# One maximum, one scaling and one reciprocal for the two heads of a pair in the grouped attention, with both divisions on ScalarE

## The chip, the cores and the metric

One core of one Trainium2 chip runs the whole program. The metric is the time of one launch in microseconds on the device, the median of several runs. TensorE (PE in the views) multiplies, VectorE (DVE) does elementwise work and reductions, ScalarE (ACT) does activations, GpSimd (POOL) has elementwise work of its own, and the queue of SyncE (SP) issues DMAs. Each engine runs its own instructions in order and meets the others through semaphores.

## The reference

Two residual stacks run on one sequence of 512 tokens of width 1024. Each of the first stack's two layers projects the normalised input to `z`, and mixes it in three ways side by side: grouped attention (8 query heads, 2 key heads, width 64), a gated recurrence in both directions, and a convolution of 31 taps. The parts that matter here, cut short:

```python
for l in range(DEPTH):                       # DEPTH = 2
    h = rms_norm(x, norm_mix[l])
    z = h @ w_in[l]
    q_a, k_a, v_a, ..., a_c, g_c = split(z)
    o_att = block_attention(q_a, k_a, v_a)   # softmax(q k^T / 8) v, no mask, each query block of 128 against 512 keys
    o_hg  = hgrn2_bidirectional(...)
    o_cv  = conformer_conv(a_c, g_c, conv_w[l], ...)   # 31 taps along the sequence, then norm and silu
    x = x + concat(o_att, o_hg, o_cv) @ w_out[l]
    x = x + square(relu(rms_norm(x) @ w_mlp_in[l])) @ w_mlp_out[l]
```

The second stack (gated feed-forwards, a latent attention called MLA and a dilated attention) follows and is not touched by the change.

## The kernel before

Activations lie transposed in SBUF, 128 features by 512 tokens a tile. Every weight is loaded in float32, split into a high part (ScalarE, `split_hi`, L413, `w_hi`) and a low part (VectorE, `split_lo`, L422, `w_lo`), and each product is three matmuls (L444, or L452 where the result has tokens on the partitions). Weights come in units through a ring of four slots.

In a mixer layer the last eight units of the projection are multiplied with other work woven between their matmuls. The function `mixer_at` writes this out by hand: 128 points, one behind each contraction step of a unit, and at each point a list of small steps. TensorE, ScalarE and VectorE each run through the same list and do their own share of every step, in that order. From point 38 to 127 the list holds the grouped attention, from 36 to 109 the convolution: per half of the channels (`t`) one gating product and 31 taps on VectorE (L1226 and L1228, a multiply-add over up to 512 columns into `conv_sum`). `split_lo` calls stand at fixed points too. At point 111 TensorE sums the convolution over the channels (L1096, `csum`), which waits for the last tap.

The attention goes in pairs of heads: 4 pairs of heads times 4 query blocks are 16 pairs per layer, numbered 0 to 15. `pair_steps` gives the order for pair `j`: `scores j`, `values j-2`, the two turns of pair `j-1`, `divide j`. For a pair,
- **scores**: TensorE writes the 128x512 scores of head 0 into bank 4 and of head 1 into bank 5 (L857), once the exponentials of the pair ahead have read them. VectorE takes each head's row maximum into `std` (L919) and scales it into `row_stats` (L921); ScalarE takes each head's exponential with its row sum into `gqa_probs` (L893);
- **divide**: VectorE inverts the sum of the second head and of the first (L928), ScalarE multiplies the second head's probabilities by the inverse (L902), VectorE the first head's (L933);
- **turn** (one per head): TensorE transposes the probabilities (L868), ScalarE copies them out into `gqa_probs_t` (L910);
- **values**: TensorE multiplies them with the values (L878); behind every fourth pair VectorE stores the result (L959, L961).

Each instruction is followed by a wait for its own end. The buffers `gqa_probs` are four, two pairs' worth. GpSimd meanwhile weighs rows of `w_mod` (L520 to L532). The MLA attention calls the same step functions with `mla_bufs`.

Of the kernel before, what the change touches and what calls it, by code (L numbers as in the profile page):

```python
# [14 lines left out]
P = 128  # L15
L = 512
D = 1024
DT = D // P
NB = L // P
# [183 lines left out]
def build(nc, io):  # L203
    ctx = ExitStack()
    with ctx:
# [58 lines left out]

        banks = [ctx.enter_context(nc.psum_tensor(f"bank{i}", [P, L], F32)) for i in range(8)]

# [618 lines left out]
        def att_act_step(act, pairs_, bufs, kind, i):  # L885
# [10 lines left out]
            elif kind == "divide":  # L896
                it = pairs_[i]["items"][1]
                act.eng.wait_ge(inv_ready.sem, inv_ready.next(act))
                for n, (_, k, c0, _) in enumerate(it["segs"]):
                    c, part = it["stat"] + n, bufs["pr"][(2 * i + 1) % 4][:, c0:c0 + k.shape[-1]]  # L900
                    signal = pn_act if n == len(it["segs"]) - 1 else act.step
                    act.eng.activation(part, part, ACT.Identity, scale=RS[:, c:c + 1]).then_inc(signal.sem, signal.add())  # L902
                    act.eng.wait_ge(signal.sem, signal.made)
            elif kind == "turn":
                j, y = divmod(i, 2)
                n = pairs_[j]["n"]
                act.eng.wait_ge(t_ready.sem, t_ready.next(act))
                if y == 0:
                    act.eng.wait_ge(pv_twin.sem, pv_twin.next(act, lag=1))
                act.eng.activation(turned_probs(bufs, j, y)[:, 0:n], turn_bank(bufs, j, y)[:, 0:n], ACT.Copy).then_inc(pt_ready.sem, pt_ready.add())  # L910
                act.eng.wait_ge(pt_ready.sem, pt_ready.made)

        def att_dve_step(dve, pairs_, bufs, kind, i, store):
            if kind == "scores":
                for y, it in enumerate(pairs_[i]["items"]):
                    segs, c = it["segs"], it["stat"]
                    dve.eng.wait_ge(s_ready.sem, s_ready.next(dve))
                    for n, (_, k, c0, _) in enumerate(segs):
                        dve.eng.tensor_reduce(STD[:, 8 + n:9 + n], banks[4 + y][:, c0:c0 + k.shape[-1]], AX.X, ALU.max).then_inc(dve.step.sem, dve.step.add())  # L919
                        dve.eng.wait_ge(dve.step.sem, dve.step.made)  # L920
                    dve.eng.tensor_scalar(NM[:, c:c + len(segs)], STD[:, 8:8 + len(segs)], -pairs_[i]["scale"], None, ALU.mult).then_inc(nmax_ready.sem, nmax_ready.add())  # L921
                    dve.eng.wait_ge(nmax_ready.sem, nmax_ready.made)
            elif kind == "divide":
                first, second = pairs_[i]["items"]
# [41 lines left out]
        def sync_all(who, name):  # L966
# [5 lines left out]
            else:  # L972
# [4 lines left out]
                else:  # L977
# [7 lines left out]
        gqa_bufs = {"pr": [at(f"gqa_probs{i}", a, [P, L]) for i, a in enumerate((u_at + 10 * K, u_at + 12 * K, u_at + 14 * K, u_at + 6 * K))],  # L985
                    "pt": [at(f"gqa_probs_t{i}", u_at + 24 * K + 2 * K * i, [P, L]) for i in range(4)], "late": ATT_HEADS * NB // 2 - 2, "one": 12}
        CONV = [at(f"conv_sum{t}", u_at + 28 * K + 2 * K * t, [P, L]) for t in range(2)]
# [905 lines left out]
        def ffn_dve(dve, i, s):  # L1893
            for part in range(3):
# [3 lines left out]
                if (i, s, part) == (1, 1, 2):  # L1898
# [10 lines left out]
        mla_bufs = {"pr": [at(f"mla_probs{i}", a, [P, L]) for i, a in enumerate((h_at + 24 * K, h_at + 26 * K, h_at + 28 * K, u_at + 30 * K))],  # L1909
                    "pt": [at(f"mla_probs_t{i}", e_at + 20 * K + 2 * K * i, [P, L]) for i in range(2)], "late": 3 * MLA_HEADS, "one": 3 * MLA_HEADS}  # L1910
        KR = at("mla_key_rope", h_at + 30 * K, [P, L])
# [928 lines left out]
```

## Time and profile before

| | |
|---|---|
| median of 3 runs | 3871.47 us (3863.55 to 3876.67) |
| profiled execution, its own time | 3871.41 us |
| its span | 3869.6 us |
| mean granted TensorE clock | 0.97 |
| TensorE busy | 3669.3 us (95%) |
| VectorE busy | 2142.9 us (55%) |
| ScalarE busy | 1350.7 us (35%) |
| GpSimd busy | 860.9 us (22%) |
| chain that ended last, shares by engine | PE 77%, DVE 17%, ACT 3%, issue 3% |

The last row follows the chain of work that ended last from its end to its start and says on which engine it ran. The shares are averages over a long program; the two mixer stages, where the change lies, are read by themselves in the rows below.

### The profile page before, as it was taken

Reading aid. Unit: us, or ns where it says so; the run is one execution under the profiler, and the core shown is the slowest. Engines: PE = TensorE matmul, PEld = TensorE weight load, DVE = VectorE, ACT = ScalarE, POOL = GpSimd, SP = SyncE. Lnnn points to the kernel's source line nnn. Section 1 sums busy time; section 2 is a strip of 40 time slices with the busy share of each in tenths; the row PEclk is TensorE's granted clock in tenths of the full one; section 3 lists DMA queues with packets and bytes.
Section 4 is the critical chain, followed back from the end, with each engine's and each line's share of the span. In section 5 each row is a group of like instructions: output and inputs, shape, how many; then the busy total and the mean of one; then the engine's idle time right before and its main releaser. Section 6 shows DMA issues by size and latency. Waiting matters only on the chain.

```text
span 3869.6 us, 48060 instructions
## 1 busy us (share of the span) xinstructions
PE 3669.3 (95%) x19016; PEld 2954.2 (76%) x19016; DVE 2142.9 (55%) x2923; ACT 1350.7 (35%) x1795; POOL 860.9 (22%) x688
## 2 busy tenths in 40 slices
PE   8888999988899999999899999999989999989998
PEld 6567888756688878887667888788868778777887
DVE  5977444487844454447567434633564655655334
ACT  4553323356333232223673222222233333332222
POOL 2200655330055526552222640000000000000000
PEclk8989999999999999999899999999999999999999
DMA  5211655421155556663224653233322122122331
GB/s 152 67 42 39 163 144 142 113 63 42 50 144 143 140 118 152 147 148 83 52 61 102 154 131 98 75 100 98 98 74 85 61 74 85 61 66 76 98 98 66
DMA packets 564250, 377.76 MB, mean 98 GB/s; under 512 B 37297, under 2 KB 561162, under 8 KB 564026
## 3 DMA queue, kind: packets, MB, share of 16 engines
q1 hardware_dynamic: 564026, 374.69, 36.6%
q8 instruction: 151, 2.47, 0.3%
q14 instruction: 73, 0.60, 0.1%
HBM read 372.45 MB, written 2.17 MB: 97 GB/s over the span
## 4 chain that ended last, share of the span: by engine, by line
PE 77%; DVE 17%; ACT 3%; issue 3%; SPq 0%; DMA 0%; DVEq 0%; ACTq 0%
PE bank L444 61%; PE bank L452 3%; DVE conv_sum L1228 3%; PE bank L487 2%; DVE w_lo L422 2%; DVE std L919 1%; PE bank L481 1%; PE bank L857 1%; PE bank L482 1%; DVE hgrn_scores L1408 1%; DVE norm_tmp L1665 1%; PE bank L2292 1%; DVE norm_tmp L1659 1%; DVE X L1661 1%; DVE H_lo L1671 1%
## 5 line engine op out<-in xcount | busy, mean ns | idle before, releaser
L444 PE MATMUL bank<-H_hi,w_hi 128*128 128x512 f32 x2384 | 969.4, 407 | 4.9 <-DVE w_lo L422 1.7
L444 PE MATMUL bank<-H_hi,w_lo 128*128 128x512 f32 x2384 | 933.7, 392 | 0.0
L444 PE MATMUL bank<-H_lo,w_hi 128*128 128x512 f32 x2384 | 933.0, 391 | 0.0
L422 DVE TENSOR_TENSOR w_lo<-w_raw,w_hi 128x2048 fp32r<-128x2048 f32 (+3 forms) x285 | 662.8, 2326 | 150.5 <-ACT w_hi L413 142.6
L413 ACT ACTIVATE w_hi<-w_raw 128x2048 fp32r<-128x2048 f32 (+3 forms) x285 | 528.9, 1856 | 308.5 <-DMA w_raw<-in_ffn_w_up 131.5
L520 POOL TENSOR_TENSOR w_mod_raw<-w_mod_raw,silu_c 128x1024 f32<-128x1024 f32 x144 | 284.9, 1978 | 1337.4 <-DMA w_mod_raw<-in_w_mod 1291.8
L444 PEld LDWEIGHTS bank<-H_hi,w_hi 128*128 128x128 f32 x2384 | 449.0, 188 | 140.8 <-issue 49.3
L444 PE MATMUL bank<-U_hi,w_hi 128*128 128x512 f32 x1376 | 540.7, 393 | 3.8 <-DVE note L963 3.7
L444 PE MATMUL bank<-U_hi,w_lo 128*128 128x512 f32 x1376 | 536.8, 390 | 0.0
L444 PE MATMUL bank<-U_lo,w_hi 128*128 128x512 f32 x1376 | 536.4, 390 | 0.0
L444 PEld LDWEIGHTS bank<-H_hi,w_lo 128*128 128x128 f32 x2384 | 448.9, 188 | 96.8 <-issue 0.3
L444 PEld LDWEIGHTS bank<-H_lo,w_hi 128*128 128x128 f32 x2384 | 449.7, 189 | 90.8 <-issue 6.7
L1802 DVE TENSOR_TENSOR U_hi<-silu_gate,bank 128x512 fp32r<-128x512 f32 x88 | 60.5, 688 | 509.8 <-PE bank L444 500.1
L444 PEld LDWEIGHTS bank<-U_hi,w_hi 128*128 128x128 f32 x1376 | 259.0, 188 | 58.6 <-issue 4.4
L444 PEld LDWEIGHTS bank<-U_hi,w_lo 128*128 128x128 f32 x1376 | 258.7, 188 | 54.1
L444 PEld LDWEIGHTS bank<-U_lo,w_hi 128*128 128x128 f32 x1376 | 259.1, 188 | 52.7
L1789 ACT ACTIVATE silu_gate<-bank 128x512 f32<-128x512 f32 x88 | 52.8, 600 | 705.4 <-PE bank L444 701.0
L522 POOL TENSOR_TENSOR w_mod_raw<-w_mod_raw 128x512 f32<-128x512 f32 x144 | 214.1, 1487 | 11.3
L524 POOL TENSOR_TENSOR w_mod_raw<-w_mod_raw 128x256 f32<-128x256 f32 x144 | 160.5, 1115 | 11.3
L481 PE MATMUL bank<-H_hi,w_hi 128*128 128x512 f32 x320 | 135.9, 425 | 21.9 <-ACT H_hi L1637 12.0
L816 ACT ACTIVATE mid<-bank 128x512 f32<-128x512 f32 x64 | 38.4, 600 | 296.2 <-PE bank L444 275.4
L774 DVE TENSOR_TENSOR X<-X,bank 128x512 f32<-128x512 f32 x64 | 44.0, 688 | 171.1 <-PE bank L444 170.5
(366 smaller groups left out, 4696.7 us busy)
## 6 DMA issues: line engine op xcount, KB each, us to landing
w_mod_raw<-in_w_mod SPq DMA_DIRECT2D x576, 128.0 KB, 5.7
w_raw<-in_ffn_w_gate SPq DMA_DIRECT2D x88, 512.0 KB, 4.0
w_raw<-in_ffn_w_up SPq DMA_DIRECT2D x88, 512.0 KB, 5.4
w_raw<-in_dil_w_in SPq DMA_DIRECT2D x36, 1024.0 KB, 5.1
w_raw<-in_w_mlp_in SPq DMA_DIRECT2D x32, 1024.0 KB, 6.0
w_raw<-in_w_mlp_out SPq DMA_DIRECT2D x32, 1024.0 KB, 5.5
w_raw<-in_ffn_w_down SPq DMA_DIRECT2D x32, 1024.0 KB, 5.0
w_raw<-in_w_in SPq DMA_DIRECT2D x16, 1024.0 KB, 5.5
```

Source lines behind the costliest of these rows:

```text
L413: act.eng.activation(WH[u % SLOTS][:, 0:n], RAW[u % SLOTS][:, 0:n], ACT.Copy).then_inc(hi_done.sem, hi_done.add())
L422: dve.eng.tensor_tensor(WL[u % SLOTS][:, 0:n], RAW[u % SLOTS][:, 0:n], WH[u % SLOTS][:, 0:n].bitcast(F32), ALU.subtract).then_inc(lo_done. ...
L444: mm = pe.eng.matmul(bank[0:m, :], w[:, k, c0:c0 + m], r[:, k, :], start=(k == 0 and i == 0), stop=(k == kt - 1 and i == 2))
L452: mm = pe.eng.matmul(bank[:, jb * m:(jb + 1) * m], r[:, k, b * P:(b + 1) * P], w[:, k, c0:c0 + m], start=(k == 0 and i == 0), stop=(k == k ...
L481: pe.eng.matmul(banks[place][0:m, :], wh[:, k], rh[:, k, :], start=(k == 0), stop=False)
L487: mm = pe.eng.matmul(banks[place][0:m, :], w[:, k], r[:, k, :], start=(k == 0 and i == 0 and not halves), stop=(k == kt - 1 and w is wh an ...
L520: pool.eng.tensor_tensor(w[:], w[:], CSIL[:, 8 * part:8 * part + 8].unsqueeze(2).to_broadcast([P, DT, P]), ALU.mult).then_inc(pool.step.se ...
L522: pool.eng.tensor_tensor(w[:, 0:4], w[:, 0:4], w[:, 4:8], ALU.add).then_inc(pool.step.sem, pool.step.add())
L524: pool.eng.tensor_tensor(w[:, 0:2], w[:, 0:2], w[:, 2:4], ALU.add).then_inc(pool.step.sem, pool.step.add())
L1228: ins = ve.scalar_tensor_tensor(CONV[t][:, c0:c1], Z[:, ZA + t, c0 + s:c1 + s], w, CONV[t][:, c0:c1], ALU.mult, ALU.add)
L1789: act.eng.activation(SG[u % 2][:], bank[:], ACT.Silu).then_inc(free.sem, free.add())
L1802: dve.eng.tensor_tensor(UH[:, t, :], SG[u % 2][:], bank[:], ALU.mult).then_inc(dve.step.sem, dve.step.add())
```

## The change

Banks 4 and 5 become one PSUM tensor `BOTH` of 128 x 2 x 512, whose halves keep their places in the list of banks. For the grouped attention (`joint` true; the MLA attention keeps its steps with `joint` false) VectorE waits until the scores of both heads are written, takes one maximum over the double bank with two results, and scales the two in one instruction; one reciprocal serves both row sums; and the first head's probabilities are multiplied by ScalarE, ahead of the second head's, in place of VectorE.

```diff
-        banks = [ctx.enter_context(nc.psum_tensor(f"bank{i}", [P, L], F32)) for i in range(8)]
+        banks = [ctx.enter_context(nc.psum_tensor(f"bank{i}", [P, L], F32)) for i in range(4)]
+        BOTH = ctx.enter_context(nc.psum_tensor("bank45", [P, 2, L], F32))
+        banks += [BOTH[:, 0, :], BOTH[:, 1, :]] + [ctx.enter_context(nc.psum_tensor(f"bank{i}", [P, L], F32)) for i in (6, 7)]
...
             elif kind == "divide":
-                it = pairs_[i]["items"][1]
                 act.eng.wait_ge(inv_ready.sem, inv_ready.next(act))
-                for n, (_, k, c0, _) in enumerate(it["segs"]):
-                    c, part = it["stat"] + n, bufs["pr"][(2 * i + 1) % 4][:, c0:c0 + k.shape[-1]]
-                    signal = pn_act if n == len(it["segs"]) - 1 else act.step
-                    act.eng.activation(part, part, ACT.Identity, scale=RS[:, c:c + 1]).then_inc(signal.sem, signal.add())
-                    act.eng.wait_ge(signal.sem, signal.made)
+                for y in (0, 1) if bufs["joint"] else (1,):
+                    it = pairs_[i]["items"][y]
+                    for n, (_, k, c0, _) in enumerate(it["segs"]):
+                        c, part = it["stat"] + n, bufs["pr"][(2 * i + y) % 4][:, c0:c0 + k.shape[-1]]
+                        signal = act.step if n < len(it["segs"]) - 1 else pn_act if y else pn_ready
+                        act.eng.activation(part, part, ACT.Identity, scale=RS[:, c:c + 1]).then_inc(signal.sem, signal.add())
+                        act.eng.wait_ge(signal.sem, signal.made)
...
         def att_dve_step(dve, pairs_, bufs, kind, i, store):
-            if kind == "scores":
+            both = [it["stat"] for it in pairs_[i]["items"]]
+            both = slice(both[0], both[1] + 1, both[1] - both[0])
+            if kind == "scores" and bufs["joint"]:
+                dve.eng.wait_ge(s_ready.sem, s_ready.next(dve, 2))
+                dve.eng.tensor_reduce(STD[:, 8:10], BOTH[:], AX.X, ALU.max).then_inc(dve.step.sem, dve.step.add())
+                dve.eng.wait_ge(dve.step.sem, dve.step.made)
+                dve.eng.tensor_scalar(NM[:, both], STD[:, 8:10], -pairs_[i]["scale"], None, ALU.mult).then_inc(nmax_ready.sem, nmax_ready.add(2))
+                dve.eng.wait_ge(nmax_ready.sem, nmax_ready.made)
+            elif kind == "scores":
...
+            elif kind == "divide" and bufs["joint"]:
+                dve.eng.wait_ge(p_ready.sem, p_ready.next(dve, 2))
+                dve.eng.reciprocal(RS[:, both], RS[:, both]).then_inc(inv_ready.sem, inv_ready.add())
+                dve.eng.wait_ge(inv_ready.sem, inv_ready.made)
```

The first place is VectorE's row in the woven part of layer 0, around pairs 2 and 3 of the attention. Before:

```order
L919 TENSOR_REDUCE std<-bank 128x1
L921 TENSOR_SCALAR row_stats<-std 128x1
L919 TENSOR_REDUCE std<-bank 128x1
L921 TENSOR_SCALAR row_stats<-std 128x1
L1228 SCALAR_TENSOR_TENSOR conv_sum_126<-Z,param_cols,conv_sum_126 128x508 x2
L1228 SCALAR_TENSOR_TENSOR conv_sum_126<-Z,param_cols,conv_sum_126 128x507 x2
L928 RECIPROCAL row_stats<-row_stats 128x1 x2
L933 TENSOR_SCALAR gqa_probs_118<-gqa_probs_118,row_stats 128x512
L1228 SCALAR_TENSOR_TENSOR conv_sum_126<-Z,param_cols,conv_sum_126 128x506
```

The same place of the changed kernel, whose lines are numbered a few higher (L921 is now the maximum, L923 the scaling, L936 the reciprocal, L1243 the tap):

```order
L921 TENSOR_REDUCE std<-bank 128x2
L923 TENSOR_SCALAR row_stats<-std 128x2
L1243 SCALAR_TENSOR_TENSOR conv_sum_126<-Z,param_cols,conv_sum_126 128x508 x2
L1243 SCALAR_TENSOR_TENSOR conv_sum_126<-Z,param_cols,conv_sum_126 128x507 x2
L936 RECIPROCAL row_stats<-row_stats 128x2
L1243 SCALAR_TENSOR_TENSOR conv_sum_126<-Z,param_cols,conv_sum_126 128x506
```

Seven instructions of the attention have become three, and the taps between them stand as they did. The second place is ScalarE's row at the end of layer 0's mixer, from the exponentials of pair 15 to the gates of the recurrence. Before:

```order
L893 ACTIVATE gqa_probs_121,row_stats<-bank,row_stats 128x512
L1163 ACTIVATE Z<-bank 128x512
L413 ACTIVATE w_hi_62<-w_raw_54 128x1536
L910 ACTIVATE gqa_probs_t_124<-bank 128x512
L910 ACTIVATE gqa_probs_t_125<-bank 128x512
L902 ACTIVATE gqa_probs_121<-gqa_probs_121,row_stats 128x512
L1158 ACT_TABLE_LOAD
L1158 ACTIVATE Z<-Z 128x512 x2
L1126 ACTIVATE U_hi<-Z 128x512 x2
L910 ACTIVATE gqa_probs_t_124<-bank 128x512
L910 ACTIVATE gqa_probs_t_125<-bank 128x512
L1131 ACT_TABLE_LOAD
```

The same place of the changed kernel, where L905 is the division:

```order
L895 ACTIVATE gqa_probs_121,row_stats<-bank,row_stats 128x512
L1178 ACTIVATE Z<-bank 128x512
L415 ACTIVATE w_hi_62<-w_raw_54 128x1536
L913 ACTIVATE gqa_probs_t_124<-bank 128x512
L913 ACTIVATE gqa_probs_t_125<-bank 128x512
L905 ACTIVATE gqa_probs_120<-gqa_probs_120,row_stats 128x512
L905 ACTIVATE gqa_probs_121<-gqa_probs_121,row_stats 128x512
L1173 ACT_TABLE_LOAD
L1173 ACTIVATE Z<-Z 128x512 x2
L1141 ACTIVATE U_hi<-Z 128x512 x2
L913 ACTIVATE gqa_probs_t_124<-bank 128x512
L913 ACTIVATE gqa_probs_t_125<-bank 128x512
```

One activation is added ahead of the one that was there, and everything behind it on ScalarE stands one place later. TensorE's row is the same in both kernels.

## Rows read from the trace of the kernel before

**Rows 1.** Chain that ended last, from 103 to 217 us: shares by line.

```profile
by line: DVE conv_sum L1228 44.1%; DVE std L919 17.2%; DVE w_lo L422 11.8%; DVE gqa_probs L933 6.9%; issue 4.6%; DVE row_stats L928 4.0%; DVE row_stats L921 4.0%; DVE U_hi L959 1.2%; DVE U_lo L961 1.2%; PE bank L857 1.0%; ACT gqa_probs L893
```

**Rows 2.** Stretches: length, busy us of PE, PEld, DVE, ACT, POOL; clock; DMA share; GB/s.

```profile
103.00:217.00 114.00, 99.32 (x575) 65.45 (x575) 106.69 (x173) 63.52 (x113) 32.55 (x24) 0.97 0.20 52
795.00:909.00 114.00, 99.28 (x574) 65.11 (x572) 106.03 (x171) 63.03 (x112) 31.38 (x22) 0.97 0.20 52
157.00:160.40 3.40, 3.38 (x7) 1.34 (x7) 3.19 (x7) 1.93 (x4) 0.00 (x0) 0.50 0.01 2
217.00:262.00 45.00, 39.01 (x254) 32.30 (x254) 23.16 (x41) 31.48 (x46) 0.00 (x0) 0.81 0.11 36
```

**Rows 3.** Who waited for whom, 103 to 217: total us, times, longest.

```profile
ACT gqa_probs L893 <- DVE row_stats L921: 27.6, 11, 6.1
ACT gqa_probs L902 <- DVE row_stats L928: 19.4, 10, 5.6
...
PE bank L857 <- ACT gqa_probs L893: 7.0, 6, 2.9
PE bank L868 <- DVE gqa_probs L933: 5.7, 3, 3.5
...
PE bank L878 <- ACT gqa_probs_t L910: 1.5, 2, 1.3
```

**Rows 4.** VectorE in order of time, one pair of layer 1.

```profile
827.97 0.69 DVE L919 TENSOR_REDUCE std<-bank 128x1 f32<-128x512 f32 x1
828.69 0.15 DVE L921 TENSOR_SCALAR row_stats<-std 128x1 f32<-128x1 f32 x1
...
829.79 3.08 DVE L1228 SCALAR_TENSOR_TENSOR conv_sum<-Z,param_cols,conv_sum 128x503 f32<-128x503 f32 x4
832.90 0.36 DVE L928 RECIPROCAL row_stats<-row_stats 128x1 f32<-128x1 f32 x2
833.30 0.48 DVE L933 TENSOR_SCALAR gqa_probs<-gqa_probs,row_stats 128x512 f32<-128x512 f32 x1
833.82 0.74 DVE L1228 SCALAR_TENSOR_TENSOR conv_sum<-Z,param_cols,conv_sum 128x501 f32<-128x501 f32 x1
```

**Rows 5.** VectorE's groups by shape, whole program: total, mean ns of one.

```profile
L928 DVE RECIPROCAL row_stats<-row_stats 128x2 f32<-128x2 f32 x16 | 2.7, 166 | 11.8 <-ACT mla_probs L893 11.5
L919 DVE TENSOR_REDUCE std<-bank 128x1 f32<-128x384 f32 x16 | 8.9, 558 | 0.5
```

**Rows 6.** VectorE's groups by shape, from 103 to 217 us.

```profile
L919 DVE TENSOR_REDUCE std<-bank 128x1 f32<-128x512 f32 x28 | 19.4, 691 | 2.9 <-PE bank L857 2.0
L422 DVE TENSOR_TENSOR w_lo<-w_raw,w_hi 128x2048 fp32r<-128x2048 f32 x5 | 13.4, 2676 | 0.2
L933 DVE TENSOR_SCALAR gqa_probs<-gqa_probs,row_stats 128x512 f32<-128x512 f32 x13 | 7.7, 594 | 0.5
```

**Rows 7.** VectorE and GpSimd in order of time, 148 to 155 us.

```profile
148.58 2.40 DVE L1228 SCALAR_TENSOR_TENSOR conv_sum<-Z,param_cols,conv_sum 128x499 f32<-128x499 f32 x1
151.02 3.25 DVE L422 TENSOR_TENSOR w_lo<-w_raw,w_hi 128x2048 fp32r<-128x2048 f32 x1
148.56 1.90 POOL L520 TENSOR_TENSOR w_mod_raw<-w_mod_raw,silu_c 128x1024 f32<-128x1024 f32 x1 [14.67 <-DMA w_mod_raw<-in_w_mod]
```

**Rows 8.** One pair of layer 0 from its scores to the next pair's.

```profile
166.11 0.69 PE L857 MATMUL bank<-k_flipped,Z 64*128 64x512 f32 x1
168.12 0.69 DVE L919 TENSOR_REDUCE std<-bank 128x1 f32<-128x512 f32 x1
170.62 0.19 ACT L893 ACTIVATION_READ_ACCUMULATOR gqa_probs<-bank,row_stats 128x1 f32 x1
172.95 0.69 PE L857 MATMUL bank<-k_flipped,Z 64*128 64x512 f32 x1
```

**Rows 9.** ScalarE in order of time, end of layer 0's mixer.

```profile
239.75 0.69 ACT L893 ACTIVATE gqa_probs<-bank,row_stats 128x512 f32<-128x512 f32 x1 [1.93 <-DVE row_stats L921]
...
245.72 0.73 ACT L902 ACTIVATE gqa_probs<-gqa_probs,row_stats 128x512 f32<-128x512 f32 x1
```

More of the change, by code:

```diff
@@ L985, in build @@
         gqa_bufs = {"pr": [at(f"gqa_probs{i}", a, [P, L]) for i, a in enumerate((u_at + 10 * K, u_at + 12 * K, u_at + 14 * K, u_at + 6 * K))],
-                    "pt": [at(f"gqa_probs_t{i}", u_at + 24 * K + 2 * K * i, [P, L]) for i in range(4)], "late": ATT_HEADS * NB // 2 - 2, "one": 12}
+                    "pt": [at(f"gqa_probs_t{i}", u_at + 24 * K + 2 * K * i, [P, L]) for i in range(4)], "late": ATT_HEADS * NB // 2 - 2, "one": 12, "joint": True}
         CONV = [at(f"conv_sum{t}", u_at + 28 * K + 2 * K * t, [P, L]) for t in range(2)]
@@ L1909, in build @@
         mla_bufs = {"pr": [at(f"mla_probs{i}", a, [P, L]) for i, a in enumerate((h_at + 24 * K, h_at + 26 * K, h_at + 28 * K, u_at + 30 * K))],
-                    "pt": [at(f"mla_probs_t{i}", e_at + 20 * K + 2 * K * i, [P, L]) for i in range(2)], "late": 3 * MLA_HEADS, "one": 3 * MLA_HEADS}
+                    "pt": [at(f"mla_probs_t{i}", e_at + 20 * K + 2 * K * i, [P, L]) for i in range(2)], "late": 3 * MLA_HEADS, "one": 3 * MLA_HEADS, "joint": False}
         KR = at("mla_key_rope", h_at + 30 * K, [P, L])
```

## The prediction

> **What bounds the kernel now.** The page's shares say that TensorE bounds the whole program and VectorE little of it, so the change has to be read in the two mixer stages, one per layer. I looked first at the chain of work that ended last, from 103 to 217 us, which is layer 0's woven part from the first scores to the channel sum of the convolution. It runs on VectorE nearly throughout: taps 44.1%, row maxima 17.2%, `w_lo` 11.8%, the first head's division 6.9%, reciprocals and scalings 4.0% each [rows 1]. The busy times say the same: of 114 us VectorE is busy for 106.7, and in the same stretch of layer 1, from 795 to 909, for 106.0 [rows 2]; what is left is mostly the gap of about 0.03 us behind each of its 173 instructions. TensorE is busy for 99.3 us by a measure that flatters it, ScalarE for 63.5. Third, the waits: ScalarE waits 27.6 us for the scaled maxima and 19.4 us for the reciprocals, and TensorE waits 7.0 us for exponentials, 5.7 us for the first head's division on VectorE and 1.5 us for turned probabilities, 14.2 us in all [rows 3]. The reader is to see one late engine, VectorE, and two that are held up by it. Behind the stretch, from 217 to 262 us, VectorE is busy for only 23.2 of 45 us [rows 2]; there the latency of single steps counts, and ScalarE has the longest queue of them.
>
> **What is removed on VectorE, per pair.** From the start of the first maximum to the next tap it is 829.79 - 827.97 = 1.82 us now [rows 4]. A maximum over 512 columns takes 0.691 us and one over 384 takes 0.558 [rows 5, 6], 1.04 ns a column, so that one over 2 x 512 columns is estimated at 0.691 + 0.53 = 1.22 us. The new block is then 1.22 + 0.03 + 0.15 + 0.03 = 1.43 us with the scaling and the gaps of [rows 4], 0.39 us less. The trace has no maximum over two banks: from below, two results in one instruction can't be cheaper than this slope gives; from above, it could cost what the block costs now, and save nothing. I take 1.22, because the slope is from the same instruction on the same memory. The divide block goes from 833.82 - 832.90 = 0.92 us [rows 4] to one reciprocal over two columns, 0.166 us [rows 5], and a gap, 0.20 us: 0.72 us less. In the stretch there are 28 maxima, so 14 score blocks, and 13 divisions [rows 6]. That is 14 x 0.39 = 5.5 us and 13 x 0.72 = 9.4 us. The 13 divisions take 0.594 us on average [rows 6], against 0.48 alone [rows 4], since some fall on work of GpSimd; 13 x 0.11 = 1.4 us goes with them. Sum: 16.3 us per layer off an engine that is full.
>
> The Trainium skill (SBUF — State Buffer, Who interferes with whom) says that a VectorE multiplication of one source in SBUF can take the port pair that it shares with GpSimd, for its whole length, and ScalarE's ports are its own. The mean of 0.594 us agrees. By that rule the removed division would also free GpSimd, whose lateness costs nothing here.
>
> **What is added on ScalarE.** One more division per pair of 0.73 us [rows 9], 0.75 with its gap, 13 x 0.75 = 9.8 us in the stretch, on an engine that is busy 63.5 of 114 us and spends 47 us in waits for VectorE [rows 2, 3]. Those waits hide it, as long as VectorE is the late one. What it does cost is latency. Both exponentials now start behind a factor that comes 1.22 + 0.03 + 0.15 = 1.40 us after the maximum began, in place of 0.69 + 0.03 + 0.15 = 0.87 for the first: 0.53 us later. The first head's division is ready as late as now (0.20 + 0.75 = 0.95 against 0.92), the second's 0.75 us later. Queued behind the divisions on ScalarE are the evacuation of the projection's banks, `w_hi` and the turned copies, on which TensorE waits. Where nothing hides the latency it shows whole: at the end of the mixer ScalarE waits for VectorE's factor of pair 15 at 239.75, then works almost without a pause through the division at 245.72 to the recurrence's gates [rows 9]. There I count 0.53 + 0.75 = 1.3 us per layer lost. The MLA attention keeps its instructions, and TensorE's row doesn't change: nothing for both.
>
> **What is late next.** Without its own waits TensorE would need 114 - 14.2 = 99.8 us for the stretch. Twice in the stretch the granted clock stood at 0.50, its lower level of 1.2 GHz, for 3.4 us behind a stall (157.0 to 160.4 is the first [rows 2]), and TensorE was busy all that time; at 2.4 GHz each would be half as long, so 96.4 us. VectorE would need 114 - 16.3 = 97.7 us. Two engines with nearly the same work can't both run full: each is held up whenever the other's lead is used up. How long a lead there is shows in one pair: its scores start at 166.11 (two rounds of matmuls, until 167.2), the maximum starts at 168.12, 0.9 us after that; the last exponential ends at 170.81, and the next scores start at 172.95 without having waited [rows 8]. So VectorE may be 2.1 + 0.9 = 3.0 us late before TensorE waits, and 2.5 us with the 0.53 us of above. Against it stand five bunches per stretch, in which a `w_lo` of 2.7 us on average [rows 6] stands between taps; the one of 148.58 to 154.27, a tap and a `w_lo` beside a GpSimd instruction, takes 5.65 us [rows 7]. I take 1 us lost per bunch, 5 us per layer; the bounds are none, and 5.65 - 3.0, or 2.6 us, each: 13 us.
>
> **The sum.** Per layer 16.3 - 5.0 = 11.3 us gained in the stretch, 1.3 us lost behind it: 10.0 us, less 0.5 us for the first pair, whose factor is late before anything hides it: 9.5 us. Two layers give 19 us. The profiled execution's own time is 3871.41 us (span 3869.6), which is the median of the runs (3871.47) to a tenth, so the sum needs no shift: 3871.4 - 19.0 = 3852 us.
>
> **The rivals.**
> - *The two engines hinder each other more.* For it speak the bunches and that the sums come out so close (96.4 and 97.7). With the 13 us of the upper bound 3.3 - 1.3 = 2.0 us per layer is left, 3867 us; in the middle, or with a maximum over two banks that costs what two do now (2 x (9.5 - 5.5) = 8 us left), 3863 us. Against it: between bunches VectorE's plain work is much less than TensorE's, so it catches up.
> - *The whole saving arrives.* Stalls and the halved clock go together, and TensorE loses nothing: 2 x (16.3 - 1.3) = 30.0 us, 3841 us. Against it: five bunches longer than the lead.
> - *ScalarE becomes the late one, and the kernel slower.* Place: the divide step in the woven part, where the second head's turn waits for two divisions in a row. Were the 0.53 + 0.75 = 1.28 us of latency exposed in each of the 14 pairs, that is 17.9 us against 16.3 saved, and 1.3 us behind the stretch: 2.9 us per layer, 3877 us. It decides from the point at which TensorE's waits for ScalarE's divisions and copies pass some 15 us per layer; over 3883 us it would need evacuations delayed too. For it: TensorE waits for turned copies even now (1.5 us) and ScalarE has no second queue. Against it: 47 us of waits that the 9.8 us added don't fill, and 2.5 us of lead per pair. The Trainium skill (ScalarE: Activation LUTs, Rules for kernel authors) says the same in its table: multiplications belong on VectorE, not on ScalarE. One instruction agrees with it (0.73 us against 0.48), but by the rule the change would cost time, and the rule doesn't know which engine has time to give.
>
> **How the numbers follow.** The forecast has 0.58, more hindrance 0.20, the whole saving 0.10, a late ScalarE 0.12. A difference below 0.3% of the time, 11.6 us, is about what can't be told from no change. Faster by more than that (below 3859.9): all of the forecast but a little, the whole saving, and a third of the second case, 0.73; slower by more: half of the last, 0.06; the rest 0.21. The range runs from 3841, the whole saving, to 3866, short of the last case and the far end of the second, which leaves out 0.18.
>
> **What would show it.** In the changed kernel's profile the maximum should read 128x2 from 128x1024 at about 1.22 us, 32 of them; the woven part of each mixer should be near 103 us long in place of 114; VectorE's busy time should be down by about 33 us in all (per pair 2.50 us of instructions become 1.54, and the stretched divisions go); TensorE's waits for exponentials and for the division should be down from 12.7 to about 5 us per layer, and ScalarE's waits for VectorE to under 30; the part behind the channel sum should be about 1.3 us longer. I am wrong if the maximum takes 1.4 us or more, if TensorE's waits are as long as before but for ScalarE, or if the stretch shrinks and the time comes back in the recurrence behind it.

## The result, and the profile after

| | before | changed |
|---|---|---|
| median | 3871.47 us (3863.55 to 3879.5, 7 runs) | 3848.76 us (3843.83 to 3858.55, 7 runs) |
| profiled execution, its own time | 3871.41 us | 3848.69 us |
| its span | 3869.6 us | 3846.9 us |
| TensorE / VectorE / ScalarE busy | 3669.3 / 2142.9 / 1350.7 us | 3664.3 / 2108.6 / 1373.2 us |

The ratio is 0.9944, with a 95% interval of 0.9933 to 0.9955: 22.7 us, or 0.6%, faster. The forecast was 3852 us, in a range from 3841 to 3866. One run of a later version (the joint negated maximum) was granted a mean clock of 0.58 and took 5768.92 us; it is left out of that version's time.

The chain that ended last in the changed kernel, from the first scores of layer 0 to the channel sum (102 to 203.3 us), by line:

```profile
by line: DVE conv_sum L1243 43.6%; DVE std L921 15.9%; DVE w_lo L424 11.4%; issue 6.6%; PE bank L446 4.7%; DVE row_stats L923 3.6%; PE bank L859 3.3%; DVE row_stats L936 2.0%; ACT gqa_probs L895 1.6%; PE bank L870 1.5%; DVE U_hi L974 1.4%; 
```

The first head's division (6.9% in [rows 1]) is gone from it, and in the places that it left stands TensorE, whose projection, scores and turns hold 9.5% now, where only its scores, at 1.0%, stood in the row shown of before. VectorE still carries most of the chain. The stretches of the changed kernel: the woven part of layer 0 and of layer 1, and behind each the piece from the channel sum to the start of the last pair's maximum (columns as in [rows 2]):

```profile
102.00:203.30 101.30, 95.41 (x575) 63.93 (x575) 93.06 (x118) 72.44 (x125) 27.80 (x24) 1.00 0.22 58
779.80:881.80 102.00, 97.07 (x573) 64.75 (x573) 93.19 (x118) 72.43 (x125) 26.99 (x22) 0.98 0.23 58
203.30:221.60 18.30, 16.32 (x112) 13.21 (x111) 6.79 (x9) 13.64 (x20) 0.00 (x0) 0.84 0.14 45
881.80:902.50 20.70, 18.72 (x114) 15.13 (x113) 6.79 (x9) 13.60 (x20) 0.46 (x1) 0.75 0.12 39
```

Cut at the same landmarks the woven parts of before are 113.9 and 114.0 us long, with VectorE busy for 106.5 and 106.4 us. So they lost 12.6 and 12.0 us, and VectorE 13.4 and 13.2 us of busy time in them. The whole span is accounted for in this way: 0.9 us less ahead of layer 0's woven part, 12.6 in it, 2.1 between its end and the start of layer 1's (576.5 us for 578.6), 12.0 in that one, and behind it 4.9 us more (2965.1 for 2960.2); together 22.7 us less.

Who waited for whom in the changed kernel, 102 to 203.3 us:

```profile
ACT gqa_probs L895 <- DVE row_stats L923: 16.7, 10, 3.9
...
ACT gqa_probs L905 <- DVE row_stats L936: 9.4, 8, 2.5
...
PE bank L859 <- ACT gqa_probs L895: 4.1, 4, 2.2
...
DVE std L921 <- PE bank L859: 2.9, 2, 2.1
```

Against [rows 3], TensorE's waits for exponentials fell from 7.0 to 4.1 us and those for a division from 5.7 to 0.4 (now on ScalarE); ScalarE's waits for VectorE fell from 47.0 to 26.1 us. VectorE itself waits 2.9 us for scores, where it was 2.0. VectorE's groups in the same stretch:

```profile
L921 DVE TENSOR_REDUCE std<-bank 128x2 f32<-128x1024 f32 x14 | 17.1, 1225 | 3.3 <-PE bank L859 2.9
L424 DVE TENSOR_TENSOR w_lo<-w_raw,w_hi 128x2048 fp32r<-128x2048 f32 x5 | 11.5, 2292 | 0.2
L923 DVE TENSOR_SCALAR row_stats<-std 128x2 f32<-128x2 f32 x14 | 3.6, 260 | 1.5
```

The joint maximum takes 1.225 us, as estimated from the slope; 32 stand in the whole program. What [rows 4] shows of a pair in before reads so in the changed kernel, VectorE in order of time:

```profile
132.33 1.23 DVE L921 TENSOR_REDUCE std<-bank 128x2 f32<-128x1024 f32 x1
133.66 0.17 DVE L923 TENSOR_SCALAR row_stats<-std 128x2 f32<-128x2 f32 x1
133.87 3.08 DVE L1243 SCALAR_TENSOR_TENSOR conv_sum<-Z,param_cols,conv_sum 128x503 f32<-128x503 f32 x4
136.98 0.17 DVE L936 RECIPROCAL row_stats<-row_stats 128x2 f32<-128x2 f32 x1
137.18 0.74 DVE L1243 SCALAR_TENSOR_TENSOR conv_sum<-Z,param_cols,conv_sum 128x501 f32<-128x501 f32 x1
```

The score block is 133.87 - 132.33 = 1.54 us (the gap behind the two-result maximum is 0.10 us, where the others are 0.03), the divide block 0.20.

### The profile page after: what moved, and what is told of

Read it like the earlier page. It is cut to its first block, busy times and chain, and to the rows that moved or that the text cites. A ratio compares the mean times of both kernels' runs of the same rounds, so it can differ in the third digit from the quotient of the medians.

```text
span 3846.9 us, 47964 instructions
## 1 busy us (share of the span) xinstructions
PE 3664.3 (95%) x19016; PEld 2955.3 (77%) x19016; DVE 2108.6 (55%) x2795; ACT 1373.2 (36%) x1827; POOL 847.9 (22%) x688
## 4 chain that ended last, share of the span: by engine, by line
PE 78%; DVE 15%; ACT 3%; issue 3%; SPq 0%; DMA 0%; DVEq 0%; ACTq 0%
PE bank L446 61%; PE bank L454 3%; DVE conv_sum L1243 2%; PE bank L489 2%; DVE w_lo L424 2%; PE bank L859 1%; PE bank L483 1%; PE bank L484 1%; DVE hgrn_scores L1423 1%; DVE norm_tmp L1680 1%; DVE std L921 1%; PE bank L2307 1%; DVE norm_tmp L1674 1%; DVE X L1676 1%; DVE H_lo L1686 1%
## 5 line engine op out<-in xcount | busy, mean ns | idle before, releaser
L424 DVE TENSOR_TENSOR w_lo<-w_raw,w_hi 128x2048 fp32r<-128x2048 f32 (+3 forms) x285 | 654.7, 2297 | 148.0 <-ACT w_hi L415 140.0
L524 POOL TENSOR_TENSOR w_mod_raw<-w_mod_raw 128x512 f32<-128x512 f32 x144 | 209.3, 1454 | 11.3
L526 POOL TENSOR_TENSOR w_mod_raw<-w_mod_raw 128x256 f32<-128x256 f32 x144 | 162.7, 1130 | 11.3
```

The source lines that it names most:

```text
L424: dve.eng.tensor_tensor(WL[u % SLOTS][:, 0:n], RAW[u % SLOTS][:, 0:n], WH[u % SLOTS][:, 0:n].bitcast(F32), ALU.subtract).then_inc(lo_done. ...
L524: pool.eng.tensor_tensor(w[:, 0:4], w[:, 0:4], w[:, 4:8], ALU.add).then_inc(pool.step.sem, pool.step.add())
L526: pool.eng.tensor_tensor(w[:, 0:2], w[:, 0:2], w[:, 2:4], ALU.add).then_inc(pool.step.sem, pool.step.add())
```

## The experiments

All edits are against the changed kernel unless said otherwise. "Woven part" is the stretch from the first scores to the channel sum, layer 0 and layer 1. Each ratio is to the kernel before, run beside it.

**Each half of the change alone.** The joint maximum and scaling without the rest:

```diff
-                for y in (0, 1) if bufs["joint"] else (1,):
+                for y in (1,):
...
-            elif kind == "divide" and bufs["joint"]:
+            elif kind == "divide" and False:
```

> Only the maximum and the scaling are joint; the division is as before (second head on ScalarE, first head on VectorE). If VectorE bounds the woven stretch (my theory), it loses 14 x 0.39 = 5.5 us of work per layer and the stretch from the first scores to the channel sum goes from 113.9 to about 109 us; with 0.5 us of latency behind it, about 10 us in all, a ratio near 0.9975. If the gain of the whole change came from the move of the division alone, the time stays within 3 us of before.

Measured: 3870.03 us beside 3870.53, ratio 0.9999 (0.9989 to 1.0008). Its woven parts:

```profile
101.90:212.20 110.30, 96.32 (x574) 63.64 (x574) 102.24 (x146) 63.09 (x112) 31.70 (x24) 1.00 0.21 53
790.70:902.10 111.40, 97.67 (x572) 64.26 (x572) 103.03 (x146) 63.24 (x112) 29.77 (x22) 0.98 0.21 53
```

And its waits in the first of them:

```profile
PE bank L859 <- ACT gqa_probs L895: 6.9, 7, 2.2
...
PE bank L870 <- DVE gqa_probs L948: 3.6, 4, 2.0
```

The woven parts are shorter by 3.6 and 2.6 us, less than the 5.5 each that the sum gave the joint maximum, and TensorE still waits 6.9 us for exponentials. Of these 6.2 us the later factor behind the woven part takes back 2.4: from the start of pair 15's first maximum to the first activation of the recurrence's gates it is 16.2 us in both layers, against 15.0 before. The remaining 3.8 us lie within the interval, which allows 4.3 us of gain and 3.1 of loss. So the joint maximum alone doesn't show in the time, though it does in the woven parts.

The joint reciprocal and both divisions on ScalarE, with the maxima per head:

```diff
-            if kind == "scores" and bufs["joint"]:
+            if kind == "scores" and False:
```

> Only the reciprocal is joint and both divisions are on ScalarE; maxima and scalings are per head as before. My theory: VectorE loses 13 x 0.72 + 1.4 = 10.8 us per layer, the stretch is about 104 us long, 0.75 us are lost behind it, and the whole is near 18 us faster, a ratio of 0.995. The two halves then add up to 28 us where both together gave 22.7, because TensorE has become a bound. If TensorE bounded already here, this half alone would give all 22.7 us; if ScalarE were the late engine, it would give under 5.

Measured: 3843.94 us (4 runs) beside 3870.53, ratio 0.9938 (0.9918 to 0.9958). Its woven parts:

```profile
102.20:204.50 102.30, 95.92 (x575) 63.63 (x574) 95.79 (x146) 72.91 (x126) 29.31 (x24) 1.00 0.22 57
779.70:881.70 102.00, 95.64 (x573) 63.36 (x572) 95.54 (x146) 72.91 (x126) 29.46 (x22) 1.00 0.23 58
```

With 2.4 to 2.7 us more VectorE work per layer than the whole change they are as long, within 1.0 us. What TensorE's matmuls waited there for exponentials, in the first of them:

```profile
PE bank L859 <- ACT gqa_probs L895: 3.1, 3, 1.2
```

This half came out lower than the whole, so both were run again side by side.

> The changed kernel itself, timed on the chip of the next two, so that they can be compared with it: 3848 us, give or take 3.

> The version with only the divisions moved, once more. If the joint maximum is worth nothing on top of the moved division, the two are within 3 us of one another; if it gave what I put down for it, 5.5 us of VectorE's work per layer, this one is 8 us or more above the changed kernel; if the later first exponential costs more than the work saved, it is below it by 2 to 5 us, as in the first look.

Measured: changed kernel 3847.96 us (6 runs), ratio 0.9943 (0.993 to 0.9956); divisions only 3846.9 us (5 runs), 0.9939 (0.9926 to 0.9952); before 3869.97. They can't be told apart. The joint reciprocal and the moved divisions carry the gain; no run has one of these two without the other.

**Is ScalarE near its limit?** One more ScalarE multiplication, by 1.0, of the first head's probabilities per pair:

```diff
                 act.eng.wait_ge(inv_ready.sem, inv_ready.next(act))
+                if bufs["joint"]:
+                    part = bufs["pr"][2 * i % 4][:]
+                    act.eng.activation(part, part, ACT.Identity, scale=1.0).then_inc(act.step.sem, act.step.add())
+                    act.eng.wait_ge(act.step.sem, act.step.made)
```

> The changed kernel with one more multiplication (by 1.0) of the first head's probabilities on ScalarE ahead of the two divisions of every pair: the suspected cost, 0.75 us of ScalarE's time and of the latency to both turns, once more. My theory: most of it lies in ScalarE's waits for VectorE; the stretch grows by 1 to 3 us and the part behind it by 0.75 us per layer, so the time is about 4 to 7 us above the changed kernel, near 3854. If ScalarE is the late engine, every pair pays 0.75 us, 10.5 us per layer in the stretch, and the time is back at 3870.

Measured: 3853.95 us, ratio 0.995 (0.9931 to 0.997). Layer 0's woven part:

```profile
102.50:205.70 103.20, 97.16 (x575) 64.85 (x575) 93.62 (x118) 80.62 (x138) 27.64 (x24) 0.98 0.22 57
```

8.2 us more ScalarE work lengthen it by 1.9 us (layer 1: 102.4 us, 0.4 more). The added latency is 0.75 us in each of the 13 pairs that it stands in there, 9.8 us; had it been exposed it would show here. The rival in which ScalarE becomes the late engine falls. The time itself says less: the interval of this run and that of the changed kernel overlap.

**Is VectorE still the bound?** From above, a maximum over a constant table added on VectorE per pair (0.69 us):

```diff
                 dve.eng.wait_ge(inv_ready.sem, inv_ready.made)
+                dve.eng.tensor_reduce(STD[:, 10:11], COS[:], AX.X, ALU.max).then_inc(dve.step.sem, dve.step.add())
+                dve.eng.wait_ge(dve.step.sem, dve.step.made)
```

> The changed kernel with one more maximum over a constant tile of 512 columns in SBUF (result unused) on VectorE behind the reciprocal of every pair, 0.69 us and a gap, 10 us per layer in the stretch. My theory: VectorE has about 3 us of waits and the hindrance left in the changed stretch of 101.3 us, so that some 7 of the 10 us show, and the time is near 3863. If TensorE alone bounds the changed stretch, under 3 us per layer show, near 3854 or less.

Measured: 3868.29 us (10 runs), ratio 0.9993 (0.9981 to 1.0006). Its woven parts:

```profile
103.00:213.50 110.50, 98.48 (x574) 65.60 (x574) 102.88 (x132) 72.37 (x125) 29.75 (x24) 0.97 0.21 53
792.40:901.90 109.50, 100.17 (x572) 67.05 (x572) 101.87 (x132) 72.37 (x125) 28.93 (x22) 0.95 0.21 54
```

Adding 9.8 us of busy time (102.88 - 93.06) and 14 gaps lengthens layer 0's part by 9.2 us and layer 1's by 7.5: upwards VectorE's work counts nearly whole. From below, 15 of the 31 taps of each half of the channels are left out, so that the convolution isn't the reference's (16 taps stay, 30 fewer instructions per layer):

```diff
-            todo = [step for t in range(2) for step in [("gated", t)] + [("tap", (t, k)) for k in order]]
+            todo = [step for t in range(2) for step in [("gated", t)] + [("tap", (t, k)) for k in order[:15] + order[-1:]]]
```

> The changed kernel with 16 of the 31 convolution taps (15 of each half of the channels left out, so the convolution is not the reference's): VectorE has 30 taps of 0.78 us, 23 us, less in each stretch and can't be the bound there. What is left is the floor of TensorE with ScalarE's latency. My theory: VectorE and TensorE are both near their floors in the changed stretch of 101.3 and 102.0 us, so the floor is at 96 to 98 us. If TensorE alone set the changed stretch, it stays at 101 to 102 us; if VectorE alone did, it falls by 15 us or more.

Measured: 3834.86 us in one run, beside 3871.81. Its woven parts, and in a second fence its chain of layer 0's part, by line:

```profile
102.70:201.50 98.80, 96.27 (x574) 65.23 (x574) 68.21 (x89) 72.35 (x125) 24.79 (x24) 0.98 0.23 60
775.20:873.70 98.50, 96.04 (x572) 65.01 (x572) 69.26 (x89) 72.36 (x125) 23.69 (x22) 0.98 0.23 60
```

```profile
by line: PE bank L446 54.8%; PE bank L859 15.2%; PE bank L880 12.4%; PE bank L870 12.1%; issue 2.7%; DVE std L921 1.2%; ACT gqa_probs L895 1.0%; PE bank L549 0.3%; DVE row_stats L923 0.3%; ACT note L664 0.2%; ACTq L891 0.0%; DVEq L920 0.0%;
```

24.9 us off VectorE shorten the part by only 2.5 us (3.5 in layer 1), and the chain has changed engines: with this order of steps 98.5 to 98.8 us is the floor, and TensorE sets it. The changed kernel stands some 3 us above it, which is all that further relief of VectorE alone can bring in a woven part.

**What stretches VectorE's work.** GpSimd's arithmetic on `w_mod` is left out during the woven parts (one copy of 128 columns in its place, so the modulation values aren't the reference's):

```diff
+            if any(lin[("z0", l)][0] <= mod_unit[m] <= lin[("zv", l)][-1] + 6 for l in range(DEPTH)):
+                if part == 0:
+                    pool.eng.wait_ge(mod_summed.sem, mod_summed.next(pool, lag=2))
+                pool.eng.tensor_copy(MODP[:, four % 2], w[:, 0]).then_inc(mod_part.sem, mod_part.add())
+                pool.eng.wait_ge(mod_part.sem, mod_part.made)
+                return
```

> The changed kernel with GpSimd's arithmetic on the w_mod tiles that arrive during the two woven parts left out (one copy of 128 columns in place of each set, so these modulation values are not the reference's). VectorE's taps and splits then find GpSimd idle. In the changed stretch of layer 0 the taps of the slowed sizes take about 8 us more than at 0.745 us each. If the bunches are what hinders the engines, the stretch falls by 3 to 6 us per layer; if TensorE's floor holds it, by under 1.5 us.

Measured: 3835.46 us in one run, beside 3871.81. Its woven parts:

```profile
101.80:200.30 98.50, 94.78 (x574) 64.04 (x574) 83.54 (x118) 72.45 (x125) 1.95 (x4) 1.00 0.23 60
775.20:873.50 98.30, 94.57 (x573) 63.84 (x573) 83.53 (x118) 72.47 (x125) 1.70 (x3) 1.00 0.23 60
```

VectorE's groups in layer 0's part, of this run:

```profile
L1249 DVE SCALAR_TENSOR_TENSOR conv_sum<-Z,param_cols,conv_sum 128x511 f32<-128x511 f32 (+14 forms) x60 | 44.7, 744 | 2.6 <-PE bank L886 0.5
L927 DVE TENSOR_REDUCE std<-bank 128x2 f32<-128x1024 f32 x14 | 17.1, 1224 | 9.1 <-PE bank L865 8.8
...
L929 DVE TENSOR_SCALAR row_stats<-std 128x2 f32<-128x2 f32 x14 | 2.4, 169 | 1.5
```

And the taps of the changed kernel in its part:

```profile
L1243 DVE SCALAR_TENSOR_TENSOR conv_sum<-Z,param_cols,conv_sum 128x511 f32<-128x511 f32 (+14 forms) x60 | 52.9, 882 | 2.1
```

Beside GpSimd's arithmetic 60 taps take 8.2 us longer and 14 scalings 1.2 us; the maxima take the same. VectorE is busy for 83.5 us without it, in place of 93.1, and the parts come down to the floor. Only the woven parts are read from this run and the one with fewer taps: their single times lie 13 to 14 us below the changed kernel's, of which the woven parts hold some 6, and seven runs of the changed kernel differ among themselves by 14.7 us.

**A better version?** The scaling can go altogether: the factor 1/8 is put on the queries once per layer and the maximum is written negated, first as one joint maximum:

```diff
-                dve.eng.tensor_reduce(STD[:, 8:10], BOTH[:], AX.X, ALU.max).then_inc(dve.step.sem, dve.step.add())
-                dve.eng.wait_ge(dve.step.sem, dve.step.made)
-                dve.eng.tensor_scalar(NM[:, both], STD[:, 8:10], -pairs_[i]["scale"], None, ALU.mult).then_inc(nmax_ready.sem, nmax_ready.add(2))
+                dve.eng.tensor_reduce(NM[:, both], BOTH[:], AX.X, ALU.max, negate=True).then_inc(nmax_ready.sem, nmax_ready.add(2))
...
+                ve.tensor_scalar(QRSTD[:, 0:32], QRSTD[:, 0:32], HEAD ** -0.5, None, ALU.mult).then_inc(qk_rstd.sem, qk_rstd.add())
...
-                    pairs_.append({"items": items, "n": L, "scale": HEAD ** -0.5, "opens": b == 0, "closes": t if b == NB - 1 else None})
+                    pairs_.append({"items": items, "n": L, "scale": 1.0, "opens": b == 0, "closes": t if b == NB - 1 else None})
```

> The changed kernel without the scaling instruction: queries carry the factor 1/8 from the reciprocal of their norm (one small instruction per layer), and the joint maximum writes the negated value straight to the exponentials' bias. Per pair VectorE loses 0.17 us and a gap, 2.8 us per layer in the stretch, and the exponentials start 0.2 us earlier. If VectorE's work still counts in full, about 5 us under the changed kernel, near 3844; if the stretch is at TensorE's floor, within 2 us of it.

Measured: 3838.2 us (median of 3 runs), ratio 0.992 (0.99 to 0.9939). Its woven parts are 98.6 and 98.3 us long; layer 0's:

```profile
102.20:200.80 98.60, 94.84 (x576) 64.00 (x575) 89.75 (x104) 72.45 (x125) 27.04 (x24) 1.00 0.23 60
```

Then with the negated maximum per head, the other edits kept:

```diff
-                dve.eng.wait_ge(s_ready.sem, s_ready.next(dve, 2))
-                dve.eng.tensor_reduce(NM[:, both], BOTH[:], AX.X, ALU.max, negate=True).then_inc(nmax_ready.sem, nmax_ready.add(2))
-                dve.eng.wait_ge(nmax_ready.sem, nmax_ready.made)
+                for y, it in enumerate(pairs_[i]["items"]):
+                    dve.eng.wait_ge(s_ready.sem, s_ready.next(dve))
+                    dve.eng.tensor_reduce(NM[:, it["stat"]:it["stat"] + 1], banks[4 + y][:], AX.X, ALU.max, negate=True).then_inc(nmax_ready.sem, nmax_ready.add())
+                    dve.eng.wait_ge(nmax_ready.sem, nmax_ready.made)
```

> As the run before it without the scaling instruction, but with one negated maximum per head in place of the joint one: against the version with only the divisions moved (3844 us) VectorE loses two scalings of 0.154 us and gaps per pair, 5 us per layer, and the first head's exponential starts 0.18 us earlier than there and 0.7 us earlier than in the changed kernel. If latency to the exponentials matters beside VectorE's work, this is the fastest of all, near 3838 us; if the stretches are at TensorE's floor, it is within 2 us of 3844.

Measured: 3837.7 us (3835.7 to 3843.63, 4 runs), ratio 0.9917 (0.99 to 0.9934). It is the lowest median of all versions that compute the whole, but by 0.5 us only, so that it can't be told from the joint form; against the changed kernel (0.9944, 0.9933 to 0.9955) the intervals just touch. Its woven parts, and in a second fence its maxima over the whole program:

```profile
102.00:200.00 98.00, 95.35 (x575) 63.76 (x574) 92.45 (x118) 72.69 (x126) 28.51 (x24) 1.00 0.24 60
775.00:872.50 97.50, 95.00 (x573) 63.54 (x572) 91.99 (x118) 72.73 (x126) 27.05 (x22) 1.00 0.23 60
```

```profile
L922 DVE TENSOR_REDUCE row_stats<-bank 128x1 f32<-128x512 f32 x64 | 44.2, 691 | 12.6 <-PE bank L859 10.5
```

The negation costs nothing (691 ns, as in [rows 6]). Against the same form of the maximum with its scaling, the parts are 2.7 and 3.7 us shorter with one joint maximum and 4.3 and 4.5 with one per head. Two maxima per pair keep VectorE busy 2.7 us longer in layer 0 than one (92.45 against 89.75) and 0.6 in layer 1, and yet the parts are 0.6 and 0.8 us shorter, and TensorE waits 2.0 and 1.8 us for exponentials in place of 2.9 in both. In these profiles, one of each version, the earlier first exponential is worth more at the floor than VectorE's time; it also takes the parts below the 98.5 us of the joint form. The times don't show it.

**The latency behind the woven part.** Against the last kernel, the first head's division of pairs 14 and 15 goes back to VectorE, which is idle there:

```diff
-                normal = pn_act if y else pn_ready
+                normal = pn_act if y else pn_dve if bufs["joint"] and pair >= 14 else pn_ready
...
-                for y in (0, 1) if bufs["joint"] else (1,):
+                for y in (0, 1) if bufs["joint"] and i < 14 else (1,):
...
+                if i >= 14:
+                    c, part = pairs_[i]["items"][0]["stat"], bufs["pr"][2 * i % 4][:]
+                    dve.eng.tensor_scalar(part, part, RS[:, c:c + 1], None, ALU.mult).then_inc(pn_dve.sem, pn_dve.add())
+                    dve.eng.wait_ge(pn_dve.sem, pn_dve.made)
```

> The version with one negated maximum per head and no scaling, in which the first head's division of the last two pairs of each layer stands on VectorE again, which has time there. The part from the channel sum to the recurrence's gates should be 0.75 us shorter per layer than in that version where the granted clock is alike, the stretch 97.5 to 98 us as there, the time near 3836 us. If ScalarE's queue is not what sets the part behind the channel sum, the time is the same, near 3838.

Measured: 3842.37 us (5 runs) beside 3869.06, ratio 0.993 (0.9916 to 0.9943). The step itself does what it should: from the start of pair 15's scores to the first activation of the recurrence's gates it takes 16.9 and 16.7 us, against 17.5 and 17.2 without it, and from pair 15's first maximum 14.7 against 15.5, the 0.75 us expected. The time doesn't show it; the two intervals overlap. What can hide it is next to be seen. Its woven part in layer 1 is the shortest seen, 97.3 us.

**How much the piece behind the channel sum varies.** The kernel before, run and profiled once more:

> The kernel before, for a second profile of the part behind the channel sum. In the profiles of the same changed kernel this part was 39.8 and 42.5 us, then 38.8 and 38.7 us, with different granted clocks. Here it should lie between 39 and 43 us as well, with a stretch of 113.9 us again; if the changed kernel is shorter there for a reason of its own, this one stays at 40 us or above in both layers at whatever clock.

It took 3874.37 us. Its pieces from the channel sum to pair 15's first maximum, one per layer:

```profile
216.70:240.10 23.40, 21.41 (x111) 17.39 (x112) 8.49 (x17) 12.06 (x17) 0.00 (x0) 0.65 0.11 35
910.70:933.10 22.40, 20.40 (x113) 16.46 (x114) 8.54 (x17) 11.91 (x17) 0.46 (x1) 0.70 0.11 36
```

And those of the changed kernel run again (3843.88 us in its profiled execution):

```profile
204.60:221.90 17.30, 15.32 (x112) 12.69 (x111) 6.79 (x9) 13.21 (x20) 0.00 (x0) 0.90 0.15 48
882.80:900.00 17.20, 15.21 (x129) 12.81 (x129) 6.79 (x9) 12.90 (x19) 0.46 (x1) 1.00 0.15 47
```

In the first profile of the changed kernel the same pieces are 18.3 and 20.7 us long, at a granted clock of 0.84 and 0.75. In the first profile of before they are 22.0 and 19.7 us, at 0.69 and 0.83. Below 0.90 length goes with clock: 17.3 us at 0.90, 18.3 at 0.84, 20.7 at 0.75, 23.4 at 0.65. At 1.00 the piece is no shorter than at 0.90 (17.2 us).

From the channel sum to the end of the gates the kernel before now took 43.6 and 42.6 us, the first above the range expected. It stayed above 40 in both layers, which had been named as the sign that the change shortens this stretch for a reason of its own. That isn't shown: the first profile of before has 39.9 us in layer 1, and with only the divisions moved the second profile has pieces of 22.1 and 21.8 us, as long as before. It isn't ruled out either, but little is left for it: 24.6 us less in the woven parts and 2 x 1.3 more behind them make 22.0 of the 22.7 us measured.

## Why the prediction was right, and where it was not

**The saving on VectorE** was put at 16.3 us per layer. Measured in layer 0, busy time fell by 13.4 us, 54 instructions fewer save their gaps (some 1.5 us), and 14 gaps behind the joint maximum grew by 0.07 us (1.0): 13.9 us. By terms: the divisions and reciprocals were right (7.7 + 4.4 us before, 2.4 now: 9.7 us, and 26 gaps, against 9.4 + 1.4). The joint maximum was mis-sized: 5.5 us, from a block of 1.43 us. It is 1.54 us, and scalings of 128x2 are stretched beside GpSimd to 260 ns on average, so that 14 x 0.28 = 3.9 us less 14 x 0.09 = 1.3 leaves 2.6 us in the changed kernel. I had priced a new instruction by its duration in quiet surroundings and given it an old one's gap. Unforeseen were 1.9 us from `w_lo`, no longer stretched here (2.676 to 2.292 us), and 1.0 us lost on the taps.

**The hindrance** was put at 5.0 us per layer. Measured are 13.9 - 12.6 = 1.3 us in layer 0. The bunches that I charged at 1 us each got shorter with `w_lo`; that this is why so little was lost is likely, but no run tests it by itself. So the stretch came out nearly right (16.3 - 5.0 = 11.3 against 12.6 and 12.0 measured) because two terms of opposite sign were both too large, which is luck. That the two engines would come out close is shown by the runs with more and with less VectorE work: 9.8 us more in layer 0 shows as 9.2, 24.9 less as 2.5. For the 96.4 us that I gave TensorE alone the shortest part seen is 97.3.

**Which edit brings it.** Here the sum was wrong. By it the joint maximum was worth 5.5 us of 16.3 per layer; alone it changes nothing that the time shows (0.9999), and taken out of the change it isn't missed (3846.9 against 3847.96 us). The runs show two reasons. The first is that it saves half of what I gave it in the changed kernel, near TensorE's floor. The second is that both exponentials start behind a later factor. With the divisions alone it is 15.8 us from pair 15's first maximum to the gates, with both edits 16.3: this 0.5 us per layer eats the 1.0 and 0.0 us by which the woven parts are shorter with both. Whether the later factor costs time inside the woven part too is less clear. TensorE's waits for exponentials stay at 6.9 us with the joint maximum alone, where the divisions alone bring them down to 3.1 in layer 0, with 4.1 for both edits; but in layer 1 they read 7.5, 3.0 and 2.7 us.

**Behind the channel sum** 1.3 us per layer were to be lost. From the start of pair 15's scores (236.61 us) to the gates' first activation (253.79) it is 17.2 us before, and 219.40 to 237.89, 18.5 us, in the changed kernel, both with the scores at the lower clock: 1.3 us. From the start of pair 15's first maximum, behind those scores, it is 15.0 us in both layers of both profiles of before, and 16.3 in three of the changed kernel's four, 16.6 in the fourth. ScalarE of the changed kernel there, to be held against [rows 9]:

```profile
223.20 0.69 ACT L895 ACTIVATE gqa_probs<-bank,row_stats 128x512 f32<-128x512 f32 x1 [1.84 <-DVE row_stats L923]
...
229.07 1.48 ACT L905 ACTIVATE gqa_probs<-gqa_probs,row_stats 128x512 f32<-128x512 f32 x2
230.56 1.28 ACT L1173 ACT_TABLE_LOAD   x1
```

The two divisions stand in a row, 1.48 us, and the queue goes on without a pause. The term was right in both layers, but the stretch as a whole doesn't show it: from the channel sum to the end of the gates it went from 42.2 to 39.8 us in layer 0 and from 39.9 to 42.5 in layer 1, with the granted clock of its first piece. The piece varies by more than the term.

**The rivals.** More hindrance is refuted by the 1.3 us (1.7 in layer 1, counted the same way). A late ScalarE is refuted by the run with more work on it: TensorE's waits for ScalarE's divisions and copies are 0.4 + 1.3 us, where the rival needed some 15 (0.9 + 1.3 in layer 1). The whole saving did arrive but for 1.3 us per layer; it was the saving that was smaller than its 3841 us asked for. The multiplication moved to ScalarE is against a rule: the Trainium skill (ScalarE: Activation LUTs, Rules for kernel authors) wants it on VectorE; the single instruction agrees (0.723 us against 0.594), the kernel doesn't (22.7 us faster, since VectorE was full and ScalarE had 47 us of waits).

**The marks that I set:** the maximum of 128x2 at 1.22 us, 32 of them (1.225, 32); a woven part near 103 us (101.3 and 102.0); VectorE's busy time down by 33 us (34.3); TensorE's two waits down to about 5 us (4.5, and 3.6 in layer 1); ScalarE's for VectorE under 30 (26.1); 1.3 us more behind the channel sum (found from pair 15's first maximum on, not in the stretch as a whole, as told).

**Open** is what decides where in the piece behind the channel sum the granted clock falls. Runs of one kernel differ there, and no experiment varied it by itself. The 0.5 us charged for the first pair was not measured by itself.

## What to carry to other kernels

Where one engine is full and its neighbour waits for it during 47 of 114 us, move whole instructions across, even at a worse price per instruction; of two edits in one change, measure each, since the one that merges instructions can pay in latency what it saves in work. Find the floor of the next engine early, by leaving work out: here it said that only some 3 us per layer were left to relief of VectorE. And put a constant factor where it is applied once per layer instead of once per pair: the woven parts lost 2.7 to 4.5 us each by it, though the time only just shows it (3837.7 us).

## What the runs showed of the hardware

- Beside GpSimd's arithmetic, multiply-adds of VectorE with two operands in SBUF took 882 ns on average for 744, and scalings of two columns 260 ns for 169; a maximum out of PSUM took 1225 ns for 1224. For the multiply-adds and the maximum this agrees with the Trainium skill (SBUF — State Buffer, Who interferes with whom), by which an instruction with two SBUF inputs contends with GpSimd's reads and a reduction doesn't. The scalings have one input, so that this rule doesn't reach them. In the changed kernel four of the 14 in layer 0's part fell on GpSimd's work and took 0.33 to 0.63 us, the ten others 0.17; scalings of one column in the kernel before took 0.15 us even where they fell on it. In all GpSimd's work cost VectorE 9.6 us of 93.1 in one woven part.
- Two results over two PSUM banks cost one VectorE maximum 1225 ns, against 691 for one bank: the slope goes on over the bank's border. The gap behind it is 0.10 us, not 0.03.
- A maximum that is written negated costs the same 691 ns.
- The piece from the channel sum to pair 15's maximum took 17.2 to 23.4 us, by how much of it was granted 1.2 GHz in place of 2.4 (mean granted clock 1.00 to 0.65, with nothing gained from 0.90 to 1.00). The two profiled executions of the changed kernel differ by 4.8 us (3848.69 and 3843.88), and these pieces by 4.5 (39.0 and 34.5 us over both layers).
